# Small products with zeros in TensorE's idle columns: an encoder layer with sparse attention and an expert lookup, on one core

## The reference, cut to what matters

```python
h = rms(x)
cq, ckv, kpe, bq, bk, bv, iq, iw, ik, ga, gb = split(h @ w_in)
o_a = latent_attention(cq, ckv, kpe)             # 8 heads
o_b = attention over the top 128 (or 72) keys chosen by an indexer   # 8 heads
x = x + (sigmoid(ga) * (o_a @ w_o_a) + sigmoid(gb) * (o_b @ w_o_b)) @ w_out
# expert lookup, per token t and head (8 heads):
s1, s2 = q[:64] @ subkeys[0], q[64:] @ subkeys[1]    # 128 keys each
e = 16 best pairs of (16 best of s1) x (16 best of s2)   # of 128 * 128 experts
g = softmax(scores of e)
out = sum over the 8 * 16 experts of  g * gelu(t . u[e]) * v[e]
x = x + out
```

## Time and profile before

| | |
|---|---|
| time, three runs | 1795.63, 1802.37, 1803.94 us; median 1802.37 |
| the profiled execution | 1796.99 us, span of its instructions 1795.2 us |
| mean granted TensorE clock | 0.787 |
| TensorE, VectorE, ScalarE, GpSimd busy | 68%, 73%, 32%, 29% |
| moved by DMA | 696.48 MB, mean 388 GB/s |
| first gather issued, last gather issued | 195.1 us, 1772.8 us |

### The profile page before, as it was taken

The page is one execution under the profiler, slowest core; times in us unless marked ns, Lnnn a source line. Parts: engine busy times, 40 slices in busy tenths (PEclk is TensorE's granted clock), DMA queues, the critical chain, the costliest instruction groups (busy, mean ns, idle before and its releaser), DMA issues.

```text
span 1795.2 us, 26399 instructions
## 1 busy us (share of the span) xinstructions
PE 1223.4 (68%) x9056; PEld 679.3 (38%) x9056; DVE 1310.8 (73%) x3857; ACT 579.7 (32%) x1995; POOL 526.2 (29%) x569
## 2 busy tenths in 40 slices
PE   8989976677867575878877666679867343434343
PEld 3668532344535232444535223356535111111111
DVE  5662696989666676989666768998766878686754
ACT  2331134333423333334323334344423222222222
POOL 0200232333322223332322223232323333333332
PEclk9989889787988696897998697887999555555555
DMA  6238699999999999999999999999999999999997
GB/s 267 74 100 294 250 422 421 422 425 425 424 424 423 417 401 383 420 425 424 425 423 422 423 407 390 426 400 398 422 424 423 427 426 426 425 427 423 427 421 294
DMA packets 119381, 696.48 MB, mean 388 GB/s; under 512 B 17983, under 2 KB 21118, under 8 KB 49102
## 3 DMA queue, kind: packets, MB, share of 16 engines
q0 software_dynamic: 78848, 570.53, 76.0%
q1 hardware_dynamic: 36686, 121.83, 17.5%
q10 hardware_dynamic: 3712, 2.43, 0.4%
HBM read 691.65 MB, written 3.02 MB: 387 GB/s over the span
## 4 chain that ended last, share of the span: by engine, by line
DMA 35%; DVE 25%; PE 25%; issue 6%; ACT 3%; POOL 1%; ACTq 0%; DVEq 0%; SPq 0%; POOLq 0%
DMA rows<-in_peer_uv,index 26%; DVE rows L2657 11%; PE ps_v L1820 5%; DMA wch<-in_w_row 4%; PE ps_f L1559 4%; PE ps_f L1353 2%; PE ps_f L1574 2%; PE ps_h L1800 2%; DMA wch<-in_peer_wq 2%; DVE score L2333 1%; PE ps_f L1477 1%; PE ps_f L1653 1%; DVE best L2332 1%; DMA wch<-in_w_ukv 1%; PE ps_f L1437 1%
## 5 line engine op out<-in xcount | busy, mean ns | idle before, releaser
L2657 DVE CUSTOM_DVE_ANT_0 rows<-rows,ps_h 128x1024 f32<-128x1024 f32 x544 | 658.0, 1220 | 289.1 <-DMA rows<-in_peer_uv,index 236.3
L1330 POOL DMA_INDIRECT rows<-in_peer_uv,index x544 | 516.4, 949 | 1169.4 <-PE ps_v L1820 988.8
L1820 PE MATMUL ps_v<-rows,diag 128*32 128x256 f32 x4352 | 419.1, 500 | 432.0 <-ACT diag L2164 424.8
L1820 PEld LDWEIGHTS ps_v<-rows,diag 128*32 128x32 f32 x4352 | 124.2, 130 | 677.5 <-ACT diag L2164 561.7
L2155 ACT ACTIVATE tan<-arg 128x2 f32<-128x2 f32 x272 | 55.3, 203 | 799.2 <-DVE arg L2667 756.4
L2158 ACT ACTIVATE weight<-tan,lead 128x1 f32<-128x1 f32 x544 | 180.8, 379 | 9.1
L2164 ACT ACTIVATE diag<-sel,weight 128x32 f32<-128x32 f32 x544 | 140.9, 306 | 0.6 <-PE ps_v L1820 0.6
L1559 PEld LDWEIGHTS ps_f<-bufh,wch 128*128 128x128 f32 x768 | 103.7, 214 | 19.9 <-issue 17.8
L1559 PE MATMUL ps_f<-bufh,wch 128*128 128x128 f32 x768 | 109.7, 302 | 0.0
L1353 PE MATMUL ps_f<-wch,bufh 128*128 128x512 f32 (+1 forms) x192 | 81.9, 565 | 27.7 <-DMA wch<-in_w_row 26.7
L1653 PE MATMUL ps_f<-bufh,wch 128*128 128x128 f32 x384 | 52.1, 293 | 12.5 <-DMA wch<-in_peer_wq 12.3
(11 more groups left out here) (398 smaller groups left out, 1682.4 us busy)
## 6 DMA issues: line engine op xcount, KB each, us to landing
wch<-in_w_gate SPq DMA_DIRECT2D x60, 512.0 KB
wch<-in_w_row SPq DMA_DIRECT2D x36, 512.0 KB
wch<-in_w_o SPq DMA_DIRECT2D x32, 512.0 KB
wch<-in_w_out SPq DMA_DIRECT2D x24, 512.0 KB
wch<-in_peer_wq SPq DMA_DIRECT2D x24, 512.0 KB
rows<-in_peer_uv,index POOLq DMA_INDIRECT x544
w_tok<-in_w_tok SPq DMA_DIRECT2D x4, 1640.0 KB, 12.9
wch<-in_w_uq SPq DMA_DIRECT2D x6, 384.0 KB
```

Source lines behind the costliest of these rows:

```text
L1330: pool.indirect_dma_start(rows[c % RING][:, :, :].rearrange("p a d -> p (a d)"), None, io.peer_uv[:, :], at).then_inc(s_uv[c % RING], 16)
L1820: ins = nc.tensor.matmul(ps_v[GROUP * a:GROUP * (a + 1), :], diag[:, c % DRING, :], rows[c % RING][:, 1, QD * a:QD * (a + 1)], start=False ...
L2657: v.tensor_tensor_reduce(out=u, in0=u, in1=ps_h[:, :], scale=1.0, scalar=0.0, op0=ALU.mult, op1=ALU.add, accum_out=dots[:, c % KEEP:c % KE ...
```

## The change

In those columns of the three looped passes where the planner gives TensorE little work, it executes up to five more products ahead of the mix. Their stationary operand is the part of `vm` with rows 0 to 111 and head 7's columns, all zeros, the moving operand the first 112 rows of `rep`; the product, 64 x 128 zeros, is added to the sums in `ps_v` that stand open at that time. How many a column gets comes from the planner's prices: as many of 0.3 us as bring TensorE's priced steps of that column up to 1.5 us, none if they are above. For this reckoning alone the price of two steps that stand for other columns' work (`HANDS`) is zero. The first nine columns of the stream have none, and the last 160 columns neither.

```diff
+LEVEL = 1.5
+FILLER = 0.3
...
-def step_work(p):
+def step_work(p, hands=HANDS):
...
-    pe_head = {5: DC * small, 8: 7 * small, 13: 3 * small, 16: 4 * 0.67 + 2 * wide, 23: 9 * small, 26: 2 * H * small, 27: HANDS}
+    pe_head = {5: DC * small, 8: 7 * small, 13: 3 * small, 16: 4 * 0.67 + 2 * wide, 23: 9 * small, 26: 2 * H * small, 27: hands}
...
         if k == 0:
-            pe += HANDS
+            pe += hands
...
+FILLERS = {}
+
+
+def fillers_at(b):
+
+    p, k = b // SLOTS + 1, b % SLOTS
+    if p >= NP or (p == 1 and k < AFTER_TILE):
+        return 0
+    if p not in FILLERS:
+        work, done, FILLERS[p] = step_work(p, 0.0), 0, []
+        for c in range(SLOTS):
+            n = ticks_at(SLOTS * (p - 1) + c)
+            busy = sum(pe for pe, _ in work[done:done + n])
+            done += n
+            FILLERS[p].append(max(0, round((LEVEL - busy) / FILLER)))
+    return FILLERS[p][k]
...
+            def fill(n):
+                rows_in, cols_in = META * (H - 1), slice(AV * (H - 1), AV * H)
+                for _ in range(n):
+                    nc.tensor.matmul(ps_v[0:AV, 0:P], vm[0:rows_in, 0, cols_in],
+                                     rep[0:rows_in, :, :].rearrange("p a m -> p (a m)"), start=False, stop=False)
...
                     if (b - LAG) % SG == 0 and b > LAG:
                         residual((b - LAG) // SG)
+                    fill(fillers_at(b))
                     mix(b - LAG)
```

## The result

The changed kernel takes 1810.13 us (median of seven runs, 1807.71 to 1818.57), the kernel before 1802.37 (seven runs, 1795.63 to 1803.94). The ratio is 1.0061 with a 95% interval of 1.0038 to 1.0084; timed once more on another chip it was 1.0087 (1.0059 to 1.0115). By the ratio the kernel became slower by some 11 us (the two medians lie 7.8 us apart), where a gain of 3 us was forecast. 1810 lies inside the stated range, on the other side of no change.

What follows compares the result with a forecast made beforehand. DMA was taken as the bound; only time short of DMA work could be won. Terms -2.3 - 2.0 - 1.4 + 0 + 0.5 (instruction fetches) + 2 gave -3.2 us, so 1799 us; 8-in-10 range 1786 to 1812.

Steps and rivals of the forecast that it cites:

- rival 3: Looped passes: zeros do not raise the clock, so filled columns outlast their DMA time; +18 us, 1820; chance 0.05.
- It fits on average, in what was idle time in wait of diagonal weights: Looped passes: TensorE's work with fillers takes 316 to 349 us of a 403 us pass, 78 to 87%.
- fillers elsewhere: Filled columns with overdue mixes: a pair's second mix comes 1.24 us later; taken as +2 us, between 0 and 14.
- five stretches: Windows at 620, 700, 1090, 1170 and 1240 us where DMA falls clearly short of 425 GB/s, lacking 16.0 us together.
- 5.7 gathers under way: Steady state: 14.19 us per gather over 2.47 us per column; a slot one or two us late starves nothing.
- rival 2: 720 to 860 and 1110 to 1240 us: fillers hold back gather slots, rounds 5% longer; +14 us, 1816; chance 0.17.
- 620 to 640: A pass's first projections, slow at 6.28 us, speed up with the clock; gain taken as 2.3 us, between 0 and 2.9.
- 1240 to 1260: TensorE busy without a gap, first half at half clock; gain taken as 2.0 us, between 0 and 3.1.
- 700 to 720: VectorE waits for TensorE's spread behind sixteen transposes and a mix; gain 1.4 us, between 0 and 1.5.
- 1170 to 1200: Clock already 0.89 and VectorE busy 29.12 of 30 us; gain taken as 0, up to 2.4 us.
- 1090 to 1110: Transposes, mixes and spread a pass later, fillers between; gain taken as 0, between -2.5 and +2.4 us.
- Rival 1: The clock heals most of the short stretches, three quarters of 16.0 us; -12 us, 1790; chance 0.20.

Runs made afterwards that it cites:

- not_due: Of the change's 832 fillers, only the 272 outside the 112 columns where TensorE idled under 0.3 us before the mix; ratio to the kernel before 0.9995.
- narrow: The change's 832 fillers, each moving 8 columns instead of 128: ratio to the kernel before 1.0157; a second such run with 1664 fillers: 1.0350.
- wide: In the change's columns half as many fillers, rounded up (497), each moving 256 columns instead of 128; ratio to the kernel before 1.0133.
- waiting_68: Planner's choice replaced by 5 fillers in each of 68 columns where TensorE had idled over 1.2 us before the mix; ratio to the kernel before 1.0007.
- tail_80: No fillers in the looped passes; 405 before first mixes of pairs in the last 160 columns; ratio to the kernel before 1.0002.
- spread_first: Kernel before without fillers; in a block's last column the next block's spread goes before that column's steps; ratio to the kernel before 1.0009.

## Why the prediction was wrong

**What held.** The way of reckoning: only time without DMA work counts, and the span moved by what the DMA fell short (14 us in the passes, less the 3.9 us ahead of them, and 0.5 us for more bytes: 10.6, measured 10.7). The number of fillers (832), the price of one (0.248 us at full clock, 1.24 for five, 2.3 at half), the instruction bytes (q8 1.18 to 1.39 MB, 0.5 us as counted), and the clock of 0.84 where 0.86 was expected: it rose although the stationary operand is all zeros, which takes rival 3 away. Of the signs named, two fell on the wrong side: TensorE's wait for diagonals went down by 118 us (424.8 to 306.4), where 150 or more were due, and VectorE's wait for the spread rose over 39.3 us, to 41.2.

**What failed: "It fits on average, in what was idle time in wait of diagonal weights".** The 424.8 us of the earlier trace rows were read as room in the passes. They are a sum over the span: 223.0 us of them lie in the last 160 columns. And 201.9 us in the passes are no room at the columns that the planner fills. It fills those whose steps it prices at nothing, but the stream runs behind its planned columns: a mix is 2.53 us behind its diagonal on average, and in the 112 columns 4.0 us. A column without steps is where TensorE catches up, and the fillers took that time.

In the terms of the sum, "fillers elsewhere" was taken as +2. Outside the five stretches the DMA of the changed kernel falls some 10 us further short than before (14 us in the passes less 3.9 us inside the five). The five stretches together were counted at -5.7 us and came out at +3.9 (19.9 us in place of 16.0). The reason given for "near 0" failed as well: the 5.7 gathers under way were read in the last 160 columns (the gather at 1449.52 us), while at 712 to 714 us the DMA of the kernel before moves 29 GB/s. There no queue covers a late slot.

So rival 2 (slots held back) is the mechanism. It was priced at 14 us in the stretches 720 to 860 and 1110 to 1240; there the DMA fell from 424 to 412 and from 416 to 406 GB/s, 4.0 and 3.1 us, half of its price, though the share of 1.01 in just these stretches had been held against it. The other half of the loss lies at 440, 710 and 1250 us. That 1810 us fell into the stated range is owed to its upper end, which was drawn to reach into rival 2, and not to the forecast's own reckoning.

**The gains.** 620 to 640: the first projections did get quicker, 3.70 us for x8 against 6.28, but five fillers stand ahead of the mixes behind them. The timeline of the changed kernel:

```profile
626.55 3.70 PE L1371 MATMUL ps_f<-wch,bufh 128*128 128x512 f32 x8 [0.81 <-DVE bufh L2252]
630.18 1.31 PE L1837 MATMUL ps_v<-rep,vm 112*64 112x128 f32 x10
631.41 0.64 PE L1844 MATMUL ps_v<-rows,diag 128*32 128x256 f32 x8
631.98 1.31 PE L1837 MATMUL ps_v<-rep,vm 112*64 112x128 f32 x10
```

The 2.6 us are spent again within two columns (1.24 us of fillers each); the window lacks the same 2.9 us (364 GB/s, before 363). 1240 to 1260, counted at -2.0, became 2.6 us worse; 700 to 720, counted at -1.4, 1.4 worse; 1170 to 1200, counted at 0, 0.7 worse (381 against 391); 1090 to 1110, counted at 0, 0.7 us better (374 against 358), with a new shortfall behind it.

**The rivals.** Rival 2 is what happened, in part at the places it named. Rival 1 did not happen: in not_due, where the fillers cost nothing, a clock of 0.87 gained nothing that can be measured. But the clock's worth need not be nil. The narrow runs, with fillers of 8 moved columns at the same places and a clock of 0.82, lost more than the change, though narrow's fillers took less of TensorE's time (127 us against 203). That suggests a loss by held-back mixes of which the higher clock paid a part back. It is not shown by itself: no run here changes the clock and nothing else, and since wide lost more than its time explains, the shape of a filler may have a cost of its own. A filler that is skipped when a mix is due was not tried; the order of instructions here is fixed beforehand.

No run here beats the kernel before; waiting_68, not_due, tail_80 and spread_first are level with it.

## What to carry to other kernels

Work that is meant to be free must stand where the engine waits in the trace, not where a plan has little for it: read the idle time right before the instruction that others wait for, by stage, and not a wait's total over the span. In a schedule that runs late, an empty place is where it catches up. And raise a clock only for an engine whose speed the bound depends on in that stretch. Here the DMA's share of 1.01 told beforehand that in most stretches it did not depend on TensorE's.

## What the runs showed of the hardware that was not expected

- At 320 to 330 us of the narrow run TensorE, with products of 8 moved columns among its work, was busy for 9.51 of 10 us by the records at a granted clock of 0.50; with 128 moved columns in the same places the clock in the passes was 0.93, with 8 it was 0.82, no higher than in the three kernels without fillers there (0.85, 0.84 and 0.83: before, tail_80 and spread_first).
- Their time depends on the clock as well: ten instructions with 8 moved columns and 64 weight columns took 1.17 us at half and 0.68 at full clock, to the start of the mix. With 128 moved columns ten took 2.3 and 1.24 us. The prediction had read from the value products that a smaller side doesn't make a product cheaper; with 8 moved columns it does.
- Products with a stationary operand of zeros raised the clock: 0.85 to 0.93 in the passes.
